# One hybrid encoder layer: finish, branches, output and feed-forward as one block, token-major mixer outputs, first feed-forward step by token halves

## The reference, cut to what matters

```
gdn  = o_g * rsqrt(mean(o_g^2 over the head) + eps) * norm_w * silu(z)
rwkv = ((o_r - mean) * rsqrt(var + eps) * lnx_w + lnx_b + bonus) * gate   # mean, var over a head of 64
sum over branches b:  total += sigmoid_gate_b * (branch_b @ w_branch_b)     # 512 -> 1024, three times
x1   = layer_norm(alpha * x + total @ w_out)
out  = layer_norm(alpha * x1 + (silu(x1 @ w_gate) * (x1 @ w_up)) @ w_down)  # 1024 -> 2816 -> 1024
```

## Time and profile before

| | us |
|---|---|
| median of 3 runs | 2146.53 (2145.28 to 2147.59) |
| the profiled execution | 2144.27 |
| its span, first to last instruction | 2142.4 |

### The profile page before, as it was taken

How to read it: one execution, slowest core, us unless ns; L and a number is a source line. 1 busy time by engine, 2 the same in 40 slices (tenths; PEclk the granted TensorE clock), 3 DMA queues, 4 the chain that set the end, 5 groups by cost and what they waited for, 6 DMA issues and landing times. The chain is left out here.

```text
span 2142.4 us, 28824 instructions
## 1 busy us (share of the span) xinstructions
PE 1976.5 (92%) x11456; PEld 1575.0 (74%) x11456; DVE 1100.6 (51%) x1351; ACT 581.8 (27%) x926; POOL 564.3 (26%) x357
## 2 busy tenths in 40 slices
PE   5998889999999997999888899599999999999995
PEld 4876668767788885777666678488888888888884
DVE  3666764566449600666668744522433434424337
ACT  2443423235321211444442221212212112121112
POOL 3211111211122322434242372422212122122113
PEclk9999989999999998999999999799999999999998
DMA  5243565135753554666364460211111111111101
GB/s 141 52 80 93 130 153 147 40 89 134 177 148 97 127 124 127 188 187 193 90 187 144 135 207 20 59 60 59 49 39 59 29 59 59 29 59 44 44 20 79
DMA packets 340405, 211.83 MB, mean 99 GB/s; under 512 B 170796, under 2 KB 310700, under 8 KB 338256
## 3 DMA queue, kind: packets, MB, share of 16 engines
q1 hardware_dynamic: 264112, 156.33, 27.4%
q10 hardware_dynamic: 75568, 54.04, 8.8%
q0 software_dynamic: 624, 0.05, 0.1%
HBM read 151.27 MB, written 59.06 MB: 98 GB/s over the span
## 5 line engine op out<-in xcount | busy, mean ns | idle before, releaser
L154 PE MATMUL bank<-xhi,w_hi 128*128 128x512 f32 x976 | 396.3, 406 | 2.9 <-DVE xlo L868 2.9
L155 PE MATMUL bank<-xlo,w_hi 128*128 128x512 f32 x976 | 387.8, 397 | 0.0
L156 PE MATMUL bank<-xhi,w_lo 128*128 128x512 f32 x976 | 387.1, 397 | 0.0
L394 POOL TENSOR_TENSOR w_lo<-w_raw,w_hi 128x1024 fp32r<-128x1024 f32 x61 | 163.0, 2673 | 640.5 <-ACT w_hi L731 640.5
L2139 DVE TENSOR_TENSOR ff_hid<-ff_hid,ff_ps_u 128x512 f32<-128x512 f32 x42 | 28.9, 687 | 416.8 <-PE ff_ps_u L156 416.8
L154 PEld LDWEIGHTS bank<-xhi,w_hi 128*128 128x128 f32 x976 | 185.0, 190 | 49.1 <-issue 3.5
L156 PEld LDWEIGHTS bank<-xhi,w_lo 128*128 128x128 f32 x976 | 184.7, 189 | 44.9
L155 PEld LDWEIGHTS bank<-xlo,w_hi 128*128 128x128 f32 x976 | 184.9, 189 | 44.7 <-issue 2.4
L2147 DVE TENSOR_TENSOR y<-y,ff_d 128x512 f32<-128x512 f32 x320 | 199.0, 682 | 0.0
L2050 POOL TENSOR_TENSOR ff_lo_down<-ff_raw_down,ff_hi_down 128x1024 fp32r<-128x1024 f32 x22 | 52.9, 2405 | 533.0 <-ACT ff_hi_down L1987 533.0
L154 PE MATMUL ff_ps_g<-x1hi,ff_hi_gate 128*128 128x512 f32 x352 | 137.8, 391 | 18.2 <-POOL ff_lo_gate L2050 18.2
(11 more groups left out here) (320 smaller groups left out, 3527.4 us busy)
## 6 DMA issues: line engine op xcount, KB each, us to landing
w_raw<-in_w_in ACTq DMA_DIRECT2D x61, 512.0 KB, 4.2
op<-opnd SPq DMA_DIRECT2D x16, 1152.0 KB, 5.6
u<-work ACTq DMA_DIRECT2D x68, 256.0 KB, 3.4
b_gate<-u SPq DMA_DIRECT2D x24, 512.0 KB, 3.8
ff_raw_gate<-in_ffn_gate SPq DMA_DIRECT2D x22, 512.0 KB, 4.0
ff_raw_up<-in_ffn_up SPq DMA_DIRECT2D x22, 512.0 KB, 5.3
ff_raw_down<-in_ffn_down SPq DMA_DIRECT2D x22, 512.0 KB, 5.8
opnd<-work SPq DMA_DIRECT2D x20, 512.0 KB, 6.2
```

Source lines behind the costliest of these rows:

```text
L154: pe.matmul(out, w_hi, x_hi, start=first, stop=False)
L155: pe.matmul(out, w_hi, x_lo, start=False, stop=False)
L156: return pe.matmul(out, w_lo, x_hi, start=False, stop=last)
L394: pool.tensor_tensor(w_lo[b][:, :, :], w_raw[b][:, :, :], as_f32(w_hi[b][:, :, :]), ALU.subtract).then_inc(w_lo_done, 1)
```

## The change

`mix_and_project` and `feed_forward` become one function, `mix_and_feed`, with one block. Inside it:

- The scan leaves all of `ps_o` with the token on the partition: the operands of RWKV's two output products change places, the delta rule's stay. One copy of 512 numbers a partition and one transfer follow (`finish`); `o_tok`, `turn_outputs` and the copy behind it go.
- The head norms are made on token-major data, where a head lies along the free dimension: `square_g`, `square_r` on ScalarE and sums on VectorE (`tensor_reduce`) give one number for token and head, so root and reciprocal work on 32 or 64 numbers a partition. Then the slabs are turned on TensorE: `turn_g`, 32 transposes, and `turn_r`, 128 products of 64x64 with an identity. What is per channel (norm_w and z; lnx_w, lnx_b, bonus, gate) follows as before.
- Loads: the token-major outputs come as four transfers of 1 MiB in 1 KiB rows (before: eight of 512 KiB in 256-byte rows), z and bonus are double-buffered, and all of the delta rule's and RWKV's inputs are issued ahead of the third branch weight.
- Feed-forward step 0 is made in four columns (gate and up, for each half of the tokens), with the last two turns between them; its weights are loaded once the first 8 output tiles are done.
- GpSimd's clear of the scan's semaphores stands behind the split of the output weights, and those of the joined function are cleared after the last block.

```
-                if c:
-                    turn_outputs(c - 1)
...
-                        pe.matmul(ps_o[h, j, :], sv[d][h, 4 * e + j, :], ar[d][h, 4 * e + j, 1, :], start=True, stop=False)
+                        pe.matmul(rwkv(j, e), ar[d][h, 4 * e + j, 1, :], sv[d][h, 4 * e + j, :], start=True, stop=False)
...
-                act.activation(o_tok[b][:, :, :], ps_o[:, 4:8, :].rearrange("p (g k) s -> p g (k s)", k=2), ACT.Copy).then_inc(o_tok_done, 1)
...
-                act.activation(o[b][:, 0:4, :], ps_o[:, 0:4, :], ACT.Copy).then_inc(o_rw_done, 1)
+                act.activation(o[b][:, :], ps_o[:, :], ACT.Copy).then_inc(o_done, 1)
...
+            load_tok(gt, 256, 0, gt_landed)
             load_w(1)
...
+            def turn_g(p):
+                for hh in range(2):
...
+                    for c in range(8):
+                        last = pe.transpose(fin[hh][:, c // 4, c % 4 * P:(c % 4 + 1) * P], gt[:, 8 * hh + c, p * P:(p + 1) * P], tab("ident"))
+                    last.then_inc(g_turned, 1)
...
+            after = {3: [(turn_g, 0)], 4: [(turn_g, 1)], 10: [(turn_r, 0)], 11: [(gates, 0)], 12: [(turn_r, 1)], 13: [(gates, 1)]}
...
+            pe.wait_ge(lo_done, 7)
+            column("gate", ps_g, 0, 0, None)
             turn_out(6)
+            pe.wait_ge(added, 15)
+            pe.wait_ge(lo_done, 8)
+            column("up", ps_u, 0, 0, mm_u)
             turn_out(7)
+            pe.wait_ge(x_lo, 16)
+            pe.wait_ge(added, 16)
+            column("gate", ps_g, 1, 0, mm_g)
+            column("up", ps_u, 1, 0, mm_u)
+            steps(pe, make, add)
...
+            for n in range(10):
+                if n == 1:
+                    split_gate_up(0, 0, 0)
+                    split_down(0, 0)
...
+            def sum_g(hh):
+                dve.wait_ge(g_squared, hh + 1)
+                dve.tensor_reduce(sums(gs, hh), squares(2), AX.X, ALU.add).then_inc(g_summed, 1)
...
+            def scale_g(_):
+                dve.wait_ge(g_root, 1)
+                step(dve.reciprocal(gs[:, :, :], gs[:, :, :]))
+                for hh in range(2):
+                    dve.tensor_tensor(eighth(gt, hh, 2), eighth(gt, hh, 2), spread(gs, hh, 2), ALU.mult).then_inc(g_scaled, 1)
...
-            before = {0: [(centre, 0), (finish_g, 0)], 2: [(centre, 1), (finish_g, 1)], 4: [(finish_g, 2)], 6: [(finish_g, 3)], 8: [(finish_r, 0)],
-                      10: [(centre, 2), (finish_r, 1)], 12: [(centre, 3), (finish_r, 2)], 14: [(finish_r, 3)]}
+            before = {1: [(sum_g, 0)], 2: [(sum_g, 1)], 3: [(scale_g, 0)], 4: [(finish_g, 0)], 5: [(sum_r, 0)], 6: [(finish_g, 1)], 7: [(centre_r, 0)],
+                      8: [(squares_r, 0)], 9: [(squares_r, 1)], 10: [(scale_r, 0)], 11: [(affine_r, 0)], 12: [(gate_r, 0)], 13: [(affine_r, 1)], 14: [(gate_r, 1)]}
```

More of the change, by code:

```diff
@@ L1504, in mix_and_project @@
[L1504 to L1508, removed]
+            tmp_sb = lambda name, shape: early.enter_context(nc.sbuf_tensor(name, shape, F32))
+            rt, tmp, bon = tmp_sb("f_rt", [P, NCH, 2 * P]), tmp_sb("f_tmp", [P, 2, T]), tmp_sb("f_bonus", [P, 2, T])
@@ new lines, in turn_r @@
+            def turn_r(q):
+                if q == 0:
+                    pe.wait_ge(g_read, 8)
+                    pe.wait_ge(r_scaled, 2)
+                for half in range(2):
+                    j = 2 * q + half
+                    if q:
+                        pe.wait_ge(r_ready, half + 1)
+                    for c in range(NCH):
+                        for e in range(2):
+                            h = rwkv_rows(e)
+                            last = pe.matmul(fin[half][h, c // 8, c % 8 * C:(c % 8 + 1) * C], rt[h, c, j * C:(j + 1) * C],
+                                             tab.tile[h, CONST_AT["ident2"][0]:CONST_AT["ident2"][0] + C], start=True, stop=True)
+                    last.then_inc(r_turned, 1)
@@ new lines, in _ @@
+            pe.wait_ge(lo_done, LAST * 3 + 7)
+            pe.wait_ge(silu_done, LAST + 1)
+            column("gate", ps_g, 0, 1, t_gate)
+            pe.wait_ge(lo_done, LAST * 3 + 8)
+            pe.wait_ge(mul_done, LAST * 2 + 2)
+            column("up", ps_u, 0, 1, t_up)
+            column("gate", ps_g, 1, 1, t_gate)
+            pe.wait_ge(lo_done, LAST * 3 + 9)
+            pe.wait_ge(hlo_done, LAST * 2 + 2)
+            pe.wait_ge(t_hlo, 1)
+            for n in range(8):
+                room(n)
+                down(n, 0)
+                down(n, 1).then_inc(t_down, 1)
@@ L1756, in _ @@
+            column("up", ps_u, 1, 1, t_up)
+            for n in range(8, 12):
+                room(n)
+                down(n, 0)
+            pe.wait_ge(t_hlo, 2)
+            for n in range(8, 12):
+                down(n, 1).then_inc(t_down, 1)
+            for n in range(12, 16):
+                room(n)
+                down(n, 0)
+                down(n, 1).then_inc(t_down, 1)
         @block.scalar
@@ new lines, in sum_r, with centre_r, squares_r @@
+            def sum_r(_):
+                for hh in range(2):
+                    dve.wait_ge(rt_landed[hh], 16)
+                    step(dve.tensor_reduce(sums(rs, hh), eighth(rt, hh, 4), AX.X, ALU.add))
+                step(dve.tensor_scalar(rs[:, :, :], rs[:, :, :], -1.0 / RD, None, ALU.mult))
+            def centre_r(_):
+                for hh in range(2):
+                    dve.tensor_tensor(eighth(rt, hh, 4), eighth(rt, hh, 4), spread(rs, hh, 4), ALU.add).then_inc(r_centred, 1)
+            def squares_r(hh):
+                dve.wait_ge(r_squared, hh + 1)
+                dve.tensor_reduce(sums(rv, hh), squares(4), AX.X, ALU.add).then_inc(r_summed, 1)
@@ L1864, in evacuate, with gate_r @@
+            def gate_r(q):
+                for half in range(2):
+                    dve.wait_ge(mm_gate, 2 * q + half + 1)
+                    dve.tensor_tensor(tmp[:, half, :], tmp[:, half, :], flat(fin[half]), ALU.mult).then_inc(r_ready, 1)
             def evacuate(q):
```

651 lines of the change are left out of this document (298 added, 353 removed).

## The result

The changed kernel takes 2120.09 us (median of 4 runs, 2117.50 to 2124.53) where the one before, run beside it, takes 2145.91 (4 runs). The ratio is 0.9882, with a 95% interval from 0.9861 to 0.9904: 25.8 us faster, where I had forecast 38.5 less, 2108, with a range up to 2119. The profiled execution took 2118.15 us, its span 2116.4.

What follows compares the result with a forecast made beforehand. TensorE, busy 92% of the span, was taken as the bound, with VectorE and GpSimd pacing parts of the branches. Gains 15.0 + 28.5 - 5.2 = 38.3 us from 2144.27 gave 2106.0, median 2108; range 2098 to 2119.

Steps and rivals of the forecast that it cites:

- the step on the orders of the branches: Finish and branches: orders hold nearly; VectorE's scaling before turn_r(0) and GpSimd's splits before tile 8 cost 3 us together.
- the one on the output part: Output part: step 0's weight splits fall on idle ScalarE and GpSimd, with some 5 us of room; no loss.
- Scan: Scan: dropping the two transposes, 0.37 us a chunk, only lengthens TensorE's wait for VectorE; 0.4 us gained, bounds 0 and 5.9.
- Start of tile 0: Finish part: tile 0 starts at 1082.4 instead of 1082.84, with 1.55 us added for TensorE's cold start.
- Wait for the third branch weight: Tile 2: weight queued behind 7.75 MiB; TensorE waits 7.0 us plus 1.55 cold start, 8.5; bounds under 1 and 21.
- the rival of early loads: Loads in 1 KiB rows run near 394 GB/s, so the sum is 8 us better: 2100; chance 0.15.
- Products and turns: Branches, TensorE: 32 transposes add 4.1 us, 128 small products 7.5, and four remaining `dot`s take 7.0.
- the rival of slow small work: Loads at 211 GB/s (12 us) or `turn_r` products further apart (62 ns each, 8 us): 2116 to 2120; chance 0.2.
- slow VectorE forms: VectorE's group sums and repeated-operand products run at the reciprocal's rate, 6.5 us per 1024 elements: 2185; chance 0.03.
- the rival's question: The merge doesn't pay: step 0's weights come late and ScalarE holds tile 1's root back: about 2134; chance 0.04.
- Boundary: Output to feed-forward, turn 5 to step 1: joining the functions and filling the gap gains 28.5 us.
- The end: After the last block: 65 more semaphore clears, at 0.077 to 0.083 us each, lose 5.2 us.

Runs made afterwards that it cites:

- Run 7: Changed kernel with eight transpositions of a constant block, results unread, added to each scan chunk where the old two stood: 2118.97 us, ratio 0.9875.
- Run 4: Changed kernel with SP's loads of RWKV's outputs, the gate's second factor and the bonus moved behind the third, fourth and fifth branch weight: 2114.19 us, ratio 0.9847.
- run 1: Changed kernel with one swap in VectorE's table: the second pair of delta-rule slabs finished ahead of RWKV's sums: 2109.57 us, ratio 0.9835.
- run 2: Changed kernel with VectorE's centring of RWKV's outputs moved from before to behind the evacuation of tile 7, nothing else: 2110.98 us (one run).
- run 3: On top of run 1, VectorE's second sum of RWKV's squares ahead of tile 8's evacuation and its scaling ahead of tile 9's: 2108.92 us, ratio 0.9832.
- run 5: Changed kernel with the split of step 0's down weight moved from the first output tile of the second half behind the last token tile: 2113.63 us, ratio 0.9852.
- run 6: Changed kernel with step 0's columns not laid between the last turns: both turns first, then the four columns: 2129.65 us, ratio 0.9923.
- run 8: Changed kernel with 41 semaphores of finish and branches cleared behind GpSimd's last feed-forward split, not after the last block: 2115.51 us, ratio 0.9856.

## Why the prediction was wrong, by its own steps

The span fell by 26.0 us where the sum had 38.3. Of the 12.3 missing, the step on the orders of the branches accounts for 9.5 and the one on the output part for 4.3; the other terms miss by 3 us or less each and in part cancel.

**Scan: right.** Chunks stay 13.14 us apart and L1273 (before L1285) waits 1.05 us a chunk for the 0.70 of the earlier trace rows; the 0.35 us between them are the turn. Run 7 shows how much more would have been free.

**Start of tile 0:** 1083.16 for 1082.4, with the clock at its lower level as forecast, and 0.6 us dearer (13.05 us for two tiles, where 12.45 was reckoned). Both lie within what executions differ by.

**Wait for the third branch weight: right mechanism, too dear.** It is 3.75 us from tile 1's end and 1.7 at the lower clock behind it, 5.5 for 8.5 and inside its bounds. The forecast's sign, a wait of 5 to 9 us, was not met. From 1080 to 1097.9, with the new 1 KiB rows among what was on the way, the DMA engines moved 370 GB/s on average (387 and 370 in the two stretches shown above), nearer the 394 in 4 KiB rows than the 267 that I took from the mean. (What the Trainium skill says of pieces of 512 B and more, DMA: Bandwidth & Descriptors, Specifications, goes with that: the step from 1 KiB to 4 KiB changed little. Its total of 435 GB/s was not reached here.) In the rate the rival of early loads was nearer; but it had the weight there by tile 1's end, and ScalarE could only begin on it at 1097.93, so the wait lies between the two. Run 4 shows that it goes when 3.25 MiB of the loads stand behind the weight. (By the queue shown with the change, 16 transfers stood ahead of it, not 15; the 7.75 MiB are right.)

**Products and turns: right.** `turn_r(1)` takes 3.9, so 7.8 for both where 7.5 was reckoned; `turn_g` 3.7 for 4.1; two gates 3.0 with 0.5 behind them, for 3.5. The 128 records of `turn_r(1)` are 0.030 us apart, where the rival of slow small work took 62 ns for each. VectorE's new forms take 2.24 to 2.3 us per 2048 elements, as reckoned. The worries over slow small work and slow VectorE forms are out.

**"The orders hold nearly ... I add 3 us for both": this step failed.** Both places were named, and both waited. But tile 8 cost 4.6 us and 2.9 of lower clock, `turn_r(0)` 3.4 and 1.55, 12.5 together for 3.0. Two terms were missing. The first: I let GpSimd's splits and VectorE's centring run side by side at their own durations, and they did not (runs 1 and 2); that is the wait at tile 8. The second: I priced the clock's fall at tile 0 and tile 2, but took the small waits at their length, and in this execution each cost about half as much again. (In run 2 such waits cost nothing in clock, so that part is partly chance.) The wait at `turn_r(0)` itself is the one that I had foreseen, only sized too small: 7.3 us of VectorE's work against a tile of 5.45 would be 1.9, and the work took 8.4 (1157.02 to 1165.44). It is as long in runs 1 and 2, and goes when VectorE has the sums and the scaling earlier (run 3). The end of tile 16 is 8.2 us late, 1214.9 for 1206.7: 0.8 and 0.6 at the start, 9.5 here, 0.5 in small gaps, less 3.0 at the weight and 0.1 at the turns (8.3 in these rounded terms). The weight's term, 3.0 too dear, hid part of the miss: without that luck the forecast would have been further off.

**"ScalarE and GpSimd, where both are idle": this failed in the same way.** I asked whether the weights' splits would come too late, the rival's question, and not what they do to the engine beside them. They are early; GpSimd's holds up VectorE, and TensorE loses 2.2 us and 1.7 at the lower clock (run 5). The room of 5 us was reckoned for splits that come late. VectorE's own path had 0.1 us, as the two rows of before show. The forecast had this stretch at no loss; it lost 4.3.

**Boundary: right** to 0.5 us, and run 6 splits it. **The end:** 4.5 for 5.2, since 95 clears take 6.9 us, 0.073 each, and not the 7.5 of the price from 53.

The forecast had given as its own sign of being wrong that TensorE waits for norms at tiles 8 to 13, and the sign was there. What is not settled: 1 to 2 us of most runs (1, 2, 3, 5, 6 and 8), whose medians and traces differ by that much; when the clock falls behind a short wait; and why executions differ by up to 6 us before tile 0.

## What to carry to other kernels

Free time on an engine is not enough to put work there: ask also which instructions of VectorE and GpSimd will then run at the same moment, and whether both read two operands from SBUF. Here they took turns, so a cheap split doubled operations that the path waits for (2.24 us to 4.46, 1.23 to 3.31), while a reduction beside the split was harmless. A wait of TensorE of 2 to 5 us should be priced with what its products may lose in clock behind it, here nothing to 2.9 us. A change in the order of a table can then be worth a rewritten stage: run 1's swap gave 8.3 us between tile 0 and tile 17, where all the change to the finish and the branches had gained 6.7.

## What I had not expected of the hardware

In these traces VectorE's and GpSimd's instructions on two operands in SBUF held each other up whole, one instruction each in turn: VectorE's 1.23 became 3.31 us and its 2.24 became 4.46, GpSimd's 2.4 became 4.43 and its 1.3 became 3.31. The clock fell behind a wait of 2.2 us with eight transpositions after it (granted 0.50 from 1324 to 1326), and in run 2 it stayed at 1.00 behind waits of 2.5 and 3.0. At times it fell only when the engine was at work again: at tile 2 the first six starts after the wait were 0.23 to 0.34 us apart, and the next seven gaps 0.43.
